# A diffusion step's head loop: the convolution's turned tiles in two PSUM banks instead of three, and pairs of w_ada moved to later places in the order

## Chip, cores and metric

One core of one Trainium2 chip runs the whole program. The metric is device microseconds of one execution, the median of three runs. An execution is also recorded by the hardware profiler; times "at 125.45" are microseconds from the start of the recorded span. Engines: PE (TensorE, matmuls and transposes), DVE (VectorE), ACT (ScalarE), POOL (GpSimd) and SP, which here only issues loads of weights.

## What is computed

One inference step of a two-layer diffusion trunk on 384 tokens (128 of context, 256 of a latent grid), width 1024, all in fp32. Cut to what matters:

```python
for l in range(DEPTH):                                   # 2 layers
    shift1, scale1, gate1, shift2, scale2, gate2 = split(silu(cond) @ w_ada[l] + b_ada[l])   # 6 x 1024, for c and c_ctx
    h = rms_norm(x) * (1 + scale1) + shift1
    q_lat, ckv, krope, conv_in, na_qkv = split(h @ w_in[l])
    o_mla = attention(8 heads of q_lat, ckv, krope)      # softmax
    o_conv = silu(layer_norm(depthwise_conv(glu(conv_in), width=31)))      # 256 channels
    o_na = neighbourhood_attention(4 heads of na_qkv)    # with a bias, softmax
    x = x + gate1 * (concat(o_mla, o_conv, o_na) @ w_out[l])
    h = rms_norm(x) * (1 + scale2) + shift2
    x = x + gate2 * grouped_moe(h)                       # 16 experts, two per token
```

## The kernel before, in words

**Order.** Every engine has its own program, written out by hand in the same order; semaphores join them. Nothing is scheduled at run time: an engine that waits holds back all that stands behind the wait in its program. Per layer the order is: norm, five stages of the input projection (`STAGES`, line 47), the first four heads turned (`turn_heads`, line 1019), then the **head loop** (PE: line 1194; ACT: 1751; DVE: 2361), then the output projection (`out_product`, 1234), the router and the experts.

**The head loop.** `GROUPS` (line 161) lists 12 heads: 8 of the latent attention, 4 of the neighbourhood one. The loop has 14 turns, i = 0 to 13. In turn i PE makes the scores of head i, turns the probabilities of head i-1 and multiplies the values of head i-2; DVE takes the maxima and normalises outputs; ACT does the exponentials and copies what PE turned. Some turns hold more: the second queries, keys and values (turn 0), further heads to be turned (3 and 7), the convolution's result turned (9, bank keys `cb`), its normalised rows turned back (11, keys `ln`), swish and first mixes (12).

**Pairs of w_ada.** The modulation's weights come in 24 pairs of 1 MB slots, 12 per layer. The first four pairs open the program. The other 20 (`LATER_PAIRS`, line 69; pairs 0 to 19 below) are fitted in between the first layer's work, since PE multiplies each with the two conditioning vectors and needs nothing else for it: `ADA_BEHIND` pairs behind each projection stage, `BEFORE_HEADS` ahead of the first heads, then one per turn (`pairs_after`, line 73; on PE `modulation`, line 1118, matmuls at line 1108). Before the change pairs 0 to 7 stand behind the stages, pair 8 before the heads, and pairs 9 to 19 in turns 0 to 10. Four pairs make a group in PSUM bank 7. When a group is full ACT copies it out (`evac_modulation`, line 1703, the copy at 1711); before or with the next pair PE turns it (`turn_group`, 1090, matmuls at 1096), and ACT copies the turned columns (1698). What is left at the end of the loop is closed by `close_modulation` (PE 1127, ACT 1691). Pairs 0 to 7 hold the rest of layer 0's modulation, 8 to 19 that of layer 1.

**The ring.** SP loads all weights in one fixed order (`ring_order`, line 124; issue at line 719) into six slots of SBUF: the load number q goes into the slot of load q-6 (before the experts) and waits until PE has used that up (`left`, line 642). The order in the ring is that in which PE uses the weights, so a pair that moves on PE moves in the ring. The four output weights OUT0 to OUT3 follow the last pair. Each is split into a high and a low part for PE: ACT's `out_high` (line 1653, cast at 1661) in the turns of `OUT_TURN` = (9, 10, 12, 12) (line 56), then DVE's `out_low` (2336, at 2339) from turn 11 on.

**PSUM banks.** `psum_plan` (line 207) lists all uses of a layer's first part in PE's order; they take the banks in rotation, seven in layer 0 (bank 7 belongs to the groups) and eight in layer 1 (line 304). PE writes a bank only when the use before it in that bank has been read (`once_free`). So a use that is dropped from the list moves every later one to another bank and behind another reader.

**The convolution.** DVE adds 31 taps (line 2278) into `conv_acc`, channels on partitions. In turn 9 PE turns it to tokens on partitions, three tiles of 128 tokens with 256 channels each, one bank per tile; DVE takes statistics (2403, 2405), POOL the root (762), and DVE normalises the three tiles from the same banks (`normalise_conv`, 2352, at 2357): in layer 0 at the end of turn 9, in layer 1 in turn 10 after the maxima.

Of the kernel before, what the change touches and what calls it, by code (L numbers as in the profile page):

```python
# [47 lines left out]
PAIRED = [js for js in STAGES if len(js) > 1]  # L48
PAIR_AT = [IN_AT[js[0]] for js in PAIRED]
PAIR_WIDTH = [sum(IN_WIDTH[j] for j in js) for js in PAIRED]  # L50
ADA_BEHIND = (2, 1, 2, 1, 2)
S_UP_AFTER = 3
OUT_SLOTS = D_MODEL // 256
OUT_PAIRS = OUT_SLOTS // 2
# [12 lines left out]

GROUP = 4
LATER_PAIRS = [(0, k) for k in range(4, PAIRS)] + [(n, k) for n in range(1, DEPTH) for k in range(PAIRS)]
AMONG_PROJ, BEFORE_HEADS = sum(ADA_BEHIND), 1  # L70


def pairs_after(n, what, i=0):
# [76 lines left out]
C_CTX, C_LAT = PAD, 2 * PAD + P  # L150
C_LEN = 3 * PAD + TOK
C_OUT = C_LEN - 2 * PAD

TAPS_BEFORE_LATENTS, TAPS_BEFORE_UP, TAPS_BEFORE_HEADS = 7, (18, 8), (21, 14)

# [51 lines left out]
def psum_plan(n):  # L207

    order = []
    open_group = []  # L210

    def pairs(which):

        for m, k in which:
            g, v = divmod(LATER_PAIRS.index((m, k)), GROUP)
            if v == 0:
                order.append(("group", g))
            order.extend([("turn", p) for p in open_group])
            open_group[:] = [g] if v == GROUP - 1 else []

    first_turns = [("n1", t, q) for t in range(2) for q in range(2)]
    if n == 0:

        for i, (m, k) in enumerate(FIRST_PAIRS):
            order += [("ada", m, k)]
            if i:
                order += [("mod", *FIRST_PAIRS[i - 1])]
            if i == len(FIRST_PAIRS) - 1:
                order += first_turns
        order += [("mod", *FIRST_PAIRS[-1])]  # L230
    else:
        order += first_turns
    for i, js in enumerate(STAGES):
        for t in range(TILES):
            order += [("proj", js[0], t)]
            if (i, t) == (0, 0):
                order += [("n1", 2, 0), ("n1", 2, 1)]
            if (i, t) == (2, 0):
                order += [("conv", 0), ("conv", 1)]
        pairs(pairs_after(n, "proj", i))  # L240
        if i == S_UP_AFTER:
            order += [("ql", 0), ("ql", 1), ("ckv",)]
            order += [("q", 0, t) for t in range(3)] + [("kv", 0, t) for t in range(4)]
    pairs(pairs_after(n, "heads"))
    order += heads_transposed(0)
    for i in range(len(GROUPS) + 2):
        if i < len(GROUPS):
            order += [("S", i, t) for t in range(3)]
        if i == 0:
            order += [("q", 1, t) for t in range(3)] + [("kv", 1, t) for t in range(4)]  # L250
        if 1 <= i <= len(GROUPS):
            order += [("PT", i - 1, 0), ("PT", i - 1, 1)]
        if i >= 2:
            order += [("O", i - 2)]
        if i == len(GROUPS):
            order += [("mix", t) for t in range(TILES)]
        if i == 3:
            order += heads_transposed(1) + [("rows",)]
        if i == 7:
            order += heads_transposed(2)  # L260
        if i == 9:
            order += [("cb", t) for t in range(3)]
        if i == 11:
            order += [("ln", 0), ("ln", 1)]
        pairs(pairs_after(n, "turn", i))
    order += [("turn", p) for p in open_group]
    order += [("out", 0, 0), ("mix", 3), ("mix", 4), ("out", 1, 0), ("shift",)]
    for t in range(1, TILES):
        for p in range(OUT_PAIRS):
            order += [("out", p, t)] + [(what, *k) for what, *k in AFTER_OUT[(t, p)] if what != "rest"]  # L270
    order += [("place",)]
    return order
# [93 lines left out]
def build(nc, wring, x_in, vec, rows, ckv_cache, kr_cache, nak_cache, nav_cache, cond, w_router,  # L366
          b_router, rope, shape_consts, na_bias, row_ids, no_token,
          y_prompt, y_sample, new_ckv, new_krope, new_nak, new_nav, h_rows, y_rows, tables, mod_dram):
    with ExitStack() as ctx:
# [253 lines left out]
        def bank_no(l, key):  # L623
            return USES[(l.n, *key)][0]
# [5 lines left out]
        def once_full(l, key):  # L630

            return bank_full[bank_no(l, key)], USES[(l.n, *key)][1] + 1

        def once_read(l, key):

            return bank_read[bank_no(l, key)], USES[(l.n, *key)][1] + 2
# [317 lines left out]
        def _(pe):  # L954

            def turn_around(l, key, parts, d=P):

                pe.wait_ge(*once_free(l, key))
                b = bank[bank_no(l, key)]
                for i, part in enumerate(parts):  # L960
                    mm = pe.transpose(b[0:d, i * P:(i + 1) * P], part, iden[:])  # L961
                mm.then_inc(bank_full[bank_no(l, key)], 1)
# [172 lines left out]
            for n in range(DEPTH):  # L1135
# [58 lines left out]
                for i in range(len(GROUPS) + 2):  # L1194
# [26 lines left out]
                    if i == 9:  # L1221

                        pe.wait_ge(sems["conv_done"], nth(l, "conv_done", 1))
                        for t in range(TILES):
                            at = 0 if t == 0 else C_LAT - PAD + (t - 1) * P
                            turn_around(l, ("cb", t), [conv_acc[:, c, at:at + P] for c in range(2)])
                    if i == 11:
                        pe.wait_ge(*once_read(l, ("cb", 2)))
                        for c in range(2):
                            turn_around(l, ("ln", c), [ln_tm[:, t, c * P:(c + 1) * P] for t in range(TILES)])  # L1230
                    modulation(l, pairs_after(n, "turn", i))
# [657 lines left out]
        def _(dve):  # L1889
# [337 lines left out]
            for n in range(DEPTH):  # L2227
# [114 lines left out]
                def mix_low(i):  # L2342
# [6 lines left out]
                        ins = dve.tensor_tensor(mixT_lo[1][:, i - 1, :], b[:, 0:TOK], mixT_hi[:, i + 3, :], ALU.subtract)  # L2349
                    ins.then_inc(bank_read[bank_no(l, ("mix", i))], 1)  # L2350

                def normalise_conv():
                    dve.wait_ge(sems["rstd_ready"], nth(l, "rstd_ready", RMS.index("conv") + 1))
                    for t in range(TILES):
                        dve.wait_ge(*once_full(l, ("cb", t)))
                        b = bank[bank_no(l, ("cb", t))]
                        dve.tensor_scalar(ln_tm[:, t, :], b[:, 0:CONV_CH], meanvar[:, t, 0:1], rstd[:, t:t + 1],
                                                ALU.subtract, ALU.mult) \
                                                    .then_inc(bank_read[bank_no(l, ("cb", t))], 1)

                for i in range(len(GROUPS) + 2):
                    if i < len(GROUPS):
# [35 lines left out]
                        out_low(3)  # L2398
                    if i == 9:
                        for t in range(TILES):  # L2400
                            dve.wait_ge(*once_full(l, ("cb", t)))
                            b = bank[bank_no(l, ("cb", t))]
                            dve.bn_stats(stats[:, t, :], b[:, 0:CONV_CH]).then_inc(sems["dve_step"], 1)
                            dve.wait_ge(sems["dve_step"], step(l))
                            dve.bn_aggr(meanvar[:, t, :], stats[:, t, :]).then_inc(sems["dve_step"], 1)
                            dve.wait_ge(sems["dve_step"], step(l))
                        dve.tensor_copy(ssum[:, 0:TILES], meanvar[:, :, 1]).then_inc(sems["dve_step"], 1)
                        dve.wait_ge(sems["dve_step"], step(l))
                        mean_squares(l, "conv", TILES, 1)
                        if n == 0:  # L2410
                            normalise_conv()
# [375 lines left out]
```

## Time and profile before

| what | value |
|---|---|
| median of 3 runs | 1071.9 us (1068.68 to 1073.7) |
| profiled execution, its own time | 1071.57 us |
| its span, first to last instruction | 1069.8 us |
| mean granted clock of TensorE | 0.97 |
| busy share of the span | PE 94%, DVE 39%, ACT 27%, POOL 13% |
| chain that ended last | PE 76%, DVE 9%, DMA 8%, ACT 3%, issue 2%, POOL 1% |
| HBM read | 307.08 MB |

How to read it: PE is busy nearly always, and most of the chain is its own work in the experts. The rest of the chain, DMA, DVE and ACT, lies in the two layers' first parts, some 0 to 294 us and 560 to 786 us. The granted clock is 1.00 for 2.4 GHz and 0.50 for 1.2 GHz; a value between is a stretch with both. In a timeline the durations of PE's matmuls overlap, so the queue's cost of a step is read from start to start.

### The profile page before, as it was taken

The numbers are of one execution on the slowest core, as the hardware profiler recorded it, in microseconds if no ns is written. First come the engines' busy times: TensorE is split into PE (matmuls) and PEld (weight loads), VectorE is DVE, ScalarE is ACT, GpSimd is POOL, SyncE is SP. The second block draws the span as 40 slices with busy tenths as digits, with TensorE's granted clock in tenths as the row PEclk, the third lists the DMA queues.
The fourth block names the chain that finished last, engine by engine and source line by source line (L and its number), as shares of the span: only waits on it lengthen the run. The fifth ranks groups of instructions, "written<-read, shape, count | busy, mean of one in ns | idle before, by whom it ended". The sixth has DMA issues, their size and how long they took to land.

```text
span 1069.8 us, 12824 instructions
## 1 busy us (share of the span) xinstructions
PE 1006.7 (94%) x4770; PEld 593.0 (55%) x4770; DVE 418.2 (39%) x861; ACT 290.9 (27%) x629; POOL 143.7 (13%) x192
## 2 busy tenths in 40 slices
PE   5899898999999999999979999889999999999975
PEld 1686556678854434444338976668874444343422
DVE  1348824586451010000136679767462100101014
ACT  2333265572111011010035337754210111101110
POOL 2200411201110000100101015201020110001000
PEclk9899989999899999999999999978999999999998
DMA  9778396864899999999981225104499999999971
GB/s 376 292 277 342 137 360 274 337 254 195 312 368 362 421 392 422 421 420 422 420 349 57 106 79 163 43 9 197 161 383 391 377 399 423 421 420 422 421 300 59
DMA packets 51376, 320.52 MB, mean 300 GB/s; under 512 B 8718, under 2 KB 8830, under 8 KB 16368
## 3 DMA queue, kind: packets, MB, share of 16 engines
q1 hardware_dynamic: 38448, 276.59, 63.9%
q0 software_dynamic: 12864, 43.08, 10.6%
q8 instruction: 40, 0.66, 0.2%
q14 instruction: 24, 0.20, 0.0%
HBM read 307.08 MB, written 21.25 MB: 307 GB/s over the span
## 4 chain that ended last, share of the span: by engine, by line
PE 76%; DVE 9%; DMA 8%; ACT 3%; issue 2%; POOL 1%; SPq 0%; DVEq 0%; POOLq 0%; ACTq 0%
PE bank L1372 26%; PE bank L1399 12%; PE bank L978 6%; PE bank L1249 5%; PE bank L996 4%; PE bank L961 3%; PE bank L1108 3%; DMA extra_ring<-wring_dram 3%; DMA y<-y_rows 2%; PE bank L1073 2%; PE bank L1039 2%; DMA ring<-wring_dram 2%; PE bank L968 2%; PE bank L1356 2%; PE bank L1285 1%
## 5 line engine op out<-in xcount | busy, mean ns | idle before, releaser
L1372 PE MATMUL bank<-ring,hgT 128*64 128x512 f32 (+1 forms) x512 | 156.4, 594 | 2.1 <-DMA ring<-wring_dram 1.6
L1372 PE MATMUL bank<-extra_ring,hgT 128*64 128x512 f32 (+1 forms) x512 | 155.9, 594 | 0.0
L1399 PE MATMUL bank<-extra_ring,hidT 128*64 128x512 f32 (+1 forms) x352 | 111.8, 624 | 9.7 <-DMA extra_ring<-wring_dram 9.7
L2533 DVE TENSOR_TENSOR sg<-bank,sg 128x512 f32<-128x512 f32 x22 | 15.2, 691 | 252.2 <-PE bank L1372 252.2
L1372 PEld LDWEIGHTS bank<-ring,hgT 128*64 128x64 f32 (+1 forms) x512 | 58.5, 157 | 87.5 <-issue 87.5
L1372 PEld LDWEIGHTS bank<-extra_ring,hgT 128*64 128x64 f32 (+1 forms) x512 | 58.3, 157 | 86.6 <-issue 86.5
L1399 PEld LDWEIGHTS bank<-extra_ring,hidT 128*64 128x64 f32 (+1 forms) x352 | 40.9, 163 | 71.4 <-issue 71.4
L2278 DVE SCALAR_TENSOR_TENSOR conv_acc<-conv_in,vecs,conv_acc 128x399 f32<-128x399 f32 x120 | 70.9, 632 | 2.1
L1108 PE MATMUL bank<-ring,cond_p 128*32 128x512 f32 x384 | 53.3, 675 | 17.0 <-DMA ring<-wring_dram 16.2
L978 PE MATMUL bank<-ring,hT 128*128 128x256 f32 x288 | 66.5, 392 | 2.6 <-DVE hT L1924 2.6
L889 POOL DMA_INDIRECT y_rows<-y,y_at x18 | 18.2, 1011 | 368.2 <-DVE y L2542 348.0
L762 POOL TENSOR_TENSOR rstd<-ms,half 128x28 f32<-128x28 f32 (+3 forms) x10 | 32.7, 3272 | 231.2 <-DVE ms L1900 231.2
L978 PEld LDWEIGHTS bank<-ring,hT 128*128 128x128 f32 x288 | 56.2, 197 | 11.6 <-DVE hT L1924 2.8
L1788 ACT COPY hgT<-bank 128x512 f32<-128x512 f32 x24 | 14.0, 585 | 167.3 <-PE bank L1356 140.4
L2542 DVE COPY y<-bank 128x512 f32<-128x512 f32 x18 | 12.4, 692 | 113.4 <-PE bank L1399 113.4
L1797 ACT ACTIVATE sg<-bank 128x512 f32<-128x512 f32 x22 | 13.1, 597 | 153.0 <-PE bank L1372 153.0
L1399 PE MATMUL bank<-ring,hidT 128*64 128x512 f32 (+1 forms) x160 | 49.6, 595 | 0.0
L1039 PE MATMUL bank<-kT,qT 96*128 96x128 f32 (+3 forms) x144 | 44.1, 441 | 0.2 <-ACT probsT L1648 0.2
L2018 DVE TENSOR_REDUCE rowmax<-bank 128x1 f32<-128x384 f32 (+1 forms) x56 | 24.8, 442 | 49.6 <-PE bank L1039 48.0
L1811 ACT COPY y<-bank 128x512 f32<-128x512 f32 x18 | 10.5, 585 | 107.6 <-PE bank L1399 107.6
L1249 PE MATMUL bank<-out_hi,mixT_hi 128*128 128x512 f32 x96 | 38.8, 404 | 1.1 <-DVE mixT_lo L2346 0.7
L1640 ACT ACTIVATE probs<-bank,negmax,qscale 128x384 f32<-128x384 f32 (+1 forms) x48 | 28.2, 594 | 34.9 <-DVE negmax L2021 34.8
(315 smaller groups left out, 1532.7 us busy)
## 6 DMA issues: line engine op xcount, KB each, us to landing
ring<-wring_dram SPq DMA_DIRECT2D x150, 1024.0 KB, 12.8
extra_ring<-wring_dram SPq DMA_DIRECT2D x108, 1024.0 KB, 17.8
y_rows<-hg POOLq DMA_DIRECT2D x6, 1024.0 KB, 6.2
kT<-mod_dram POOLq DMA_DIRECT2D x4, 1024.0 KB, 9.8
late<-y_rows POOLq DMA_DIRECT2D x4, 1024.0 KB, 15.5
ring<-wring_dram SPq DMA_DIRECT2D x4, 832.0 KB, 19.5
h_rows<-h_tok POOLq DMA_DIRECT2D x6, 512.0 KB, 6.2
ring<-wring_dram SPq DMA_DIRECT2D x4, 640.0 KB, 11.1
```

What stands on the lines that cost most here:

```text
L762: pool.tensor_tensor(rstd[:, 0:n], ms[:, 0:n], half[:].broadcast_to([P, n]), ALU.pow) \
L961: mm = pe.transpose(b[0:d, i * P:(i + 1) * P], part, iden[:])
L978: mm = pe.matmul(b[:, 0:n], hT[:, c, t * P:(t + 1) * P], w[:, c, :], start=(c == 0), stop=(c == KC - 1))
L996: mm = pe.matmul(b[:, 0:n], a, w, start=((c, k) == (0, 0)), stop=((c, k) == (KC - 1, 2)))
L1039: mm = pe.matmul(b[:, 0:hi - lo], qT[0:d, s, h, t * P:(t + 1) * P], kT[0:d, s, h, lo:hi], start=True, stop=True)
L1108: mm = pe.matmul(bank[b][32 * i:32 * (i + 1), :], cond_p[:, s % 2 * 4 + i, at:at + 32], w[:, i, :], start=first, stop=last)
L1249: mm = pe.matmul(b[:, :], a, w, start=((c, k) == (0, 0)), stop=((c, k) == (KC - 1, 2)))
L1372: mm = pe.matmul(b[lo:hi, :], hgT[:, 4 * i + c, lo:hi], in_ring(l, expert_slot(place, s + i))[:, c * 512:(c + 1) * 512], start=((i, c) == ...
L1399: mm = pe.matmul(b[m][lo:hi, :], hidT[:, u % 2, 2 * i + c, lo:hi], in_ring(l, expert_slot(place, 4 + i))[:, at:at + 512], start=((i, c) == ...
L1640: act.activation(out, b[:, 0:hi - lo], ACT.Exp, bias=negmax[:, g, t:t + 1], scale=qscale[:, p, 4 * t + h:4 * t + h + 1] if p < 2 else 1.0, ...
L2018: dve.tensor_reduce(rowmax[:, t:t + 1], b[:, 0:n], AX, ALU.max).then_inc(sems["dve_step"], 1)
L2278: ins = dve.scalar_tensor_tensor(conv_acc[:, c, :], conv_in[:, c, k:k + C_OUT], tap, conv_acc[:, c, :], ALU.mult, ALU.add)
```

## The change

In layer 0 the pairs are placed otherwise. One pair instead of two stands behind the fifth stage (pair 6), none before the heads, and pairs 7 to 19 stand in turns 0 to 12. So pair 7 goes from the fifth stage to turn 0, pair 8 from before the heads to turn 1, and each of pairs 9 to 19 two turns later than before. Groups close and are turned later with them: group 1 (pairs 4 to 7) is turned in turn 1 instead of before the heads, group 2 in turn 5 instead of 3, group 3 in turn 9 instead of 7, group 4 after the loop as before, but it is full only in turn 12 instead of 10. In the ring the loads move alike. `OUT_TURN` stays.

In both layers the convolution's three turned tiles take two banks: tiles 0 and 1 share `cb 0`, tile 2 has `cb 1`. PE's six transposes and DVE's work are the same; DVE waits for the bank of the tile, and frees the first bank after tile 1, the second after tile 2.

```diff
-ADA_BEHIND = (2, 1, 2, 1, 2)
+ADA_BEHIND = (2, 1, 2, 1, 1)
...
-AMONG_PROJ, BEFORE_HEADS = sum(ADA_BEHIND), 1
+AMONG_PROJ, BEFORE_HEADS = sum(ADA_BEHIND), 0
...
+CONV_ROWS = (0, C_LAT - PAD, C_LAT - PAD + P)
...
         if i == 9:
-            order += [("cb", t) for t in range(3)]
+            order += [("cb", 0), ("cb", 1)]
...
                         pe.wait_ge(sems["conv_done"], nth(l, "conv_done", 1))
-                        for t in range(TILES):
-                            at = 0 if t == 0 else C_LAT - PAD + (t - 1) * P
-                            turn_around(l, ("cb", t), [conv_acc[:, c, at:at + P] for c in range(2)])
+                        for k, ts in enumerate(((0, 1), (2,))):
+                            turn_around(l, ("cb", k), [conv_acc[:, c, CONV_ROWS[t]:CONV_ROWS[t] + P] for t in ts for c in range(2)])
                     if i == 11:
-                        pe.wait_ge(*once_read(l, ("cb", 2)))
+                        pe.wait_ge(*once_read(l, ("cb", 1)))
...
+                def turned_conv(t):
+                    dve.wait_ge(*once_full(l, ("cb", t // 2)))
+                    return bank[bank_no(l, ("cb", t // 2))][:, t % 2 * CONV_CH:(t % 2 + 1) * CONV_CH]
+
                 def normalise_conv():
                     dve.wait_ge(sems["rstd_ready"], nth(l, "rstd_ready", RMS.index("conv") + 1))
                     for t in range(TILES):
-                        dve.wait_ge(*once_full(l, ("cb", t)))
-                        b = bank[bank_no(l, ("cb", t))]
-                        dve.tensor_scalar(ln_tm[:, t, :], b[:, 0:CONV_CH], meanvar[:, t, 0:1], rstd[:, t:t + 1],
-                                                ALU.subtract, ALU.mult) \
-                                                    .then_inc(bank_read[bank_no(l, ("cb", t))], 1)
+                        ins = dve.tensor_scalar(ln_tm[:, t, :], turned_conv(t), meanvar[:, t, 0:1], rstd[:, t:t + 1],
+                                                ALU.subtract, ALU.mult)
+                        if t:
+                            ins.then_inc(bank_read[bank_no(l, ("cb", t - 1))], 1)
...
                         for t in range(TILES):
-                            dve.wait_ge(*once_full(l, ("cb", t)))
-                            b = bank[bank_no(l, ("cb", t))]
-                            dve.bn_stats(stats[:, t, :], b[:, 0:CONV_CH]).then_inc(sems["dve_step"], 1)
+                            dve.bn_stats(stats[:, t, :], turned_conv(t)).then_inc(sems["dve_step"], 1)
```

## Rows read from the trace of the kernel before

**Rows 1.** Chain that ended last, in order of time, layer 0: start us, us, what.
```profile
125.45 0.33 SPq L719
...
125.83 8.69 DMA ring<-wring_dram
...
134.56 1.93 PE bank L1108 x8
...
138.30 4.48 PE bank L961 x28
...
155.60 0.33 PE bank L961 x3
```
**Rows 2.** Stretches: us, busy PE, PEld, DVE, ACT, POOL, PEclk, DMA share, GB/s.
```profile
130.00:134.50 4.50, 1.06 (x8) 0.16 (x8) 2.75 (x5) 0.00 (x0) 4.50 (x10) 0.97 1.03 360
136.00:142.00 6.00, 6.00 (x35) 5.45 (x32) 0.00 (x0) 2.69 (x7) 0.00 (x0) 0.58 1.00 318
694.00:696.00 2.00, 2.00 (x10) 1.44 (x11) 0.36 (x1) 2.00 (x6) 0.00 (x0) 0.50 0.94 383
714.00:726.00 12.00, 12.00 (x48) 10.19 (x48) 5.71 (x12) 4.87 (x12) 0.00 (x0) 0.50 0.00 0
```
**Rows 3.** Timeline, layer 1: start us, us, engine, line, operation [idle before, its releaser].
```profile
693.32 4.07 PE L961 MATMUL bank<-shapes,qk 128*64 128x128 f32 x18 [1.44 <-ACT probs L1640]
...
711.96 1.45 DVE L2357 TENSOR_SCALAR squares<-bank,meanvar,rstd 128x256 f32<-128x256 f32 x3
...
712.64 1.51 PE L1073 MATMUL bank<-proj,probsT 128*128 128x64 f32 x6 [2.93 <-DVE squares L2357]
...
715.79 3.35 PE L1039 MATMUL bank<-kT,qT 64*128 64x128 f32 x6
...
727.02 1.28 ACT L1770 ACT_TABLE_LOAD   x1
```
**Rows 4.** Timeline, layer 0, around the first heads and turns.
```profile
120.70 12.12 DVE L2278 SCALAR_TENSOR_TENSOR conv_acc<-conv_in,vecs,conv_acc 128x399 f32<-128x399 f32 x20
...
125.35 3.64 PE L1108 MATMUL bank<-ring,cond_p 128*32 128x512 f32 x32
...
153.38 1.78 PE L1039 MATMUL bank<-kT,qT 96*128 96x128 f32 x6
...
177.67 1.06 PE L1096 MATMUL bank<-four,xn 128*128 128x8 f32 x8
```
**Rows 5.** Line 719, the six ring loads issued from 125 to 130 us: issue to landing.
```profile
DMA to landing us min/median/max: 4.7/13.4/20.0
```
**Rows 6.** Line 719, the two ring loads issued from 210 to 215 us (OUT0, OUT1).
```profile
DMA to landing us min/median/max: 4.8/5.6/6.4
```
**Rows 7.** Timeline, layer 0, turns 8 to 13 and the start of the output projection.
```profile
211.28 1.92 PE L1108 MATMUL bank<-ring,cond_p 128*32 128x512 f32 x16
...
219.70 1.91 ACT L1661 CAST out_hi<-ring 128x2048 fp32r<-128x2048 f32 x1
...
224.40 1.93 PE L1108 MATMUL bank<-ring,cond_p 128*32 128x512 f32 x16
...
225.88 0.37 ACT L1640 ACTIVATE probs<-bank,negmax 128x128 f32<-128x128 f32 x1 [4.27 <-DVE negmax L2023]
226.25 1.78 PE L1039 MATMUL bank<-kT,qT 64*128 64x128 f32 x6
...
230.55 0.39 ACT L1640 ACTIVATE probs<-bank,negmax 128x128 f32<-128x128 f32 x1
...
233.95 1.28 ACT L1770 ACT_TABLE_LOAD   x1
...
238.45 0.48 PE L1249 MATMUL bank<-out_hi,mixT_hi 128*128 128x512 f32 x1
...
241.76 0.26 ACT L1698 COPY modT<-bank 128x16 f32<-128x16 f32 x2
...
244.16 0.47 PE L1249 MATMUL bank<-out_hi,mixT_hi 128*128 128x512 f32 x1 [0.67 <-DVE mixT_lo L2346]
```

## The prediction

> **What bounds the kernel now.** I read the chain of waits in order of time first, then the granted clock by stretches, then the timelines of the stretches that the change touches. The first layer has one long hole. PE ends the last projection at 125.4 us; SP issues the next ring loads at 125.45, because their slots held that projection's weights; and PE is on the chain again only at 134.56, with the second half of pair 8 [rows 1]. The reader should see two prices there: 8.69 us of waiting for a load, and behind it 28 transposes that take 4.48 us, where three take 0.33 elsewhere [rows 1]. The clock says why: through the hole PE is busy 1.06 of 4.5 us, and from 136 to 142 it is granted 0.58, most of it the lower level (1.2 GHz) [rows 2]. The second layer has a smaller hole: PE waits 2.93 us in turn 10 for the convolution's normalised tile on DVE [rows 3], and runs at 0.50 from 714 to 726 [rows 2].
>
> **Part 1: the early wait goes.** Today pairs 6 and 7 take 3.64 us from 125.35, so a pair costs 1.85 of PE's queue (its 1.92 in a timeline overlaps its neighbours) [rows 4]. Afterwards only pair 6 stands before the first heads, and its load is already there: PE is free at 127.2. The 28 transposes no longer follow a hole, so I price them at the full clock, 28 x 0.11 = 3.1 us (bounds 3.1 and today's 4.48 [rows 1]): 130.3. The scores of turn 0, queries and keys keep today's 8.9 us (they start 0.2 before the heads' modelled end, 138.30 + 4.48, and end where pair 9 starts, 153.38 - 1.85 [rows 1, 4]): 139.2. Pair 7 now stands there, so turn 1's scores start at 141.05 against 153.38, a lead of **12.3 us**. Group 1's turn (8 matmuls, 1.06 [rows 4], some 1.0 of PE's queue) moves from before the heads into turn 1: lead 11.3. Groups 2 and 3 are turned two turns later as well, so the lead swings between 11.3 and 12.3, which changes no sum; ACT's copy of each group moves with it, into its idle time. The cover: DVE ends its taps at 132.8 [rows 4], 1.9 us after the first scores would be ready; queries and keys (7.3 us) hide that. Without them 1.9 would be lost.
> Four ring loads leave at 125.45 to 127.5 instead of six. Six needed 4.7 to 20.0 us to land [rows 5]; pair 8's second half is wanted 18 us after its issue, pair 9's later. Lower bound: the slowest, 2 us lost; I take none, since two of the six are gone. SP's order is otherwise the same, and nothing on POOL's queue moves.
>
> **Part 2: the output weights come late.** This is the added wait. OUT0 is loaded into the slot of pair 17's first half. Today that is turn 8: the pair starts at 211.28 [rows 7], the load leaves 1.1 us later and lands in 4.8 us, OUT1 behind it in 6.4 [rows 6], and ACT's split of OUT0 in turn 9 starts at 219.70 without a wait [rows 7]. The split stays in turn 9, but pair 17 goes to turn 10. Then:
> - ACT reaches the split at 219.70 - 12.3 = 207.4.
> - Pair 17 starts where pair 19 does today, 224.40 - 11.3 = 213.1 [rows 7]; issue 214.2; landed 219.0. ACT stands **11.6 us** (13.2 by the slower landing; I take the faster, as OUT0 is again the first of its two).
> - Queued behind it on ACT: the copy of group 3's turn (0.25), the exponentials of turn 10, OUT1's split. The split and the copy end at 221.1; those exponentials start at 225.88 today [rows 7]. The lead left is 4.8.
> - Who waits: PE. Turn 11's first scores get the bank of group 3's turn, which ACT reads only then. PE idles from 214.9 to 221.1, 6.2 us.
>
> **Part 3: what moved to turns 11 and 12.** At the full clock: turn 11's scores start at 221.1, their exponentials 4.3 us later as today (226.25 to 230.55 [rows 7]): 225.4, lead 5.1. The probabilities are there at 226.95; pair 18 now lies ahead of their transposes and ends at 226.2 + 1.85 = 228.05 instead, so the lead is 4.2. OUT2 and OUT3, issued behind pair 18 at 227.3 and 228.3, land at 232.1 and 234.7, just in time for ACT. Pair 19 hides in turn 12 behind ACT. But group 4's copy now stands behind all of ACT's splits and copies, which end at 241.76 today [rows 7]: 237.5, and a copy of 512 columns (a quarter of a split's 1.91), 238.0. PE must turn the group (1.0) before the output projection, which so starts at 239.1 against 238.45; its second block starts at 244.2 against 244.16 [rows 7]. **At the full clock the whole lead is spent: 0.**
> The clock is the unknown. A 6.2 us hole is longer than the one behind which the rows show 0.58. If turn 11 runs at the lower level for as long as that stretch (some 7 us), pair 18 starts 2.6 us later (scores 1.65, transposes 0.85, values 1.0, less 0.9 of waits that were there), and the second block at 246.9: +2.7. If the fall lasts until pair 18 is done (rest of the values and transposes, the pair's 1.85 twice): +6.0. PE's 2.9 us wait for group 4 (its values end at 235.2) can start another fall under the output projection: half of 7 us, 0 to +3.4. So the first layer gives 0 to +9.4; I take **+4**, nearest to the 136 to 142 row: 2.7, and 1.3 for the second fall.
> The first two loads of expert weights leave after pair 19, so two turns later; they are wanted only after the router, a whole output projection on: 0.
>
> **Part 4: two banks.** The six transposes, the statistics and the normalising stay; only bank and release change. In the first layer that is nothing (0.1 us: the first statistics wait for four transposes instead of two). In the second, where no pairs are, the rotation of eight is one step shorter: the values in turn 10 get the bank of turn 9's values, long read, instead of the convolution's first tile. They start 2.93 us earlier, at 709.7 [rows 3]. But the next scores now take the convolution's banks, the first free after the second normalised tile, 711.96 + two thirds of 1.45 = 712.9 [rows 3]. The wait moves and shrinks from 2.93 to 1.8; the scores start at 713.0 against 715.79 [rows 3], 2.8 sooner. If the clock still falls, the rest keeps its pace: 2.2 to 2.8 gained. If it stays full, layer 0's own distance from these scores to the table load of the swish holds, 226.25 to 233.95 = 7.7 us [rows 7]: 720.7 against 727.02 [rows 3], 6.3 gained. A wait of 1.44 us was already followed by 0.50 in this layer [rows 2, 3], so I take **-2.5**.
> The Trainium skill (TensorE: Matmul & The Clock Gate, HAM oscillation) has the clock fall after gaps that are long enough, and so it would rather keep it in the second layer: that result is the 6.3 just worked out. The trace's 1.44 us case speaks against it.
>
> **Sum.** The profiled execution took 1071.57 us, its span 1069.8 and 1.8 around it; it lies 0.3 below the median of 1071.9. 1071.57 + 4 - 2.5 + 0.3 = 1073.4; I say **1073**.
>
> **Rivals.**
> - *Slower.* ACT's wait for OUT0 drags a long low clock with it; this decides from the point where the fall outlasts pair 18. +9.4 - 2.2 = +7: 1079. For it: in the second layer the low clock held for 12 us of the same small matmuls (0.50 from 714 to 726 [rows 2]). Against: pairs 18 and 19 are long dense matmuls that layer 1 doesn't have. 0.25.
> - *Faster.* The clock holds in the second layer and recovers at once in the first: 0 - 6.3, 1065.5. For it: the remaining wait is 1.8 instead of 2.93. Against: the 1.44 us case. 0.13. The Trainium skill's rule (same page and section) would make this the outcome for the second layer, though not for the first.
> - *It doesn't do what it says.* The early wait returns in turn 1, because pair 8's second half lands after 20 us or more [rows 5]: 2 to 3 us of the lead lost, 1076. For it: the small bias loads share the engines then. Against: two megabytes less in front. 0.07.
>
> **How the numbers follow.** About 0.5% (5.4 us) is what a measurement of this kernel can tell from no change. My forecast (0.55) and the third rival (0.07) lie within it: 0.62 the same, 0.13 faster, 0.25 slower. The range leaves out part of each outer rival, under a fifth in all: 1066 to 1080.
>
> **What would show it.** Right: no PE wait after the last projection in layer 0, turn 1's scores near 141; ACT idle over 10 us before OUT0's split, released by the ring's load; PE idle some 6 us before turn 11's scores and a low clock behind; in layer 1 the wait in turn 10 gone from the values and standing before turn 11's scores. Wrong: ACT not waiting for OUT0 at all (then over 7 us faster); pairs 7 to 9 waiting for their loads; the output projection of layer 0 starting before 235 or after 249.

## The result, and the profile after

The change made the kernel **slower**: 1079.26 us, median of 8 runs, against 1072.7 us for the kernel before, run beside it; ratio 1.0069, 95% interval 1.0036 to 1.0102. The time lies in the forecast's range (1066 to 1080), but the forecast was 1073, within what a measurement can tell from no change. What came is the rival called *Slower*, which gave 1079.

| | before | after |
|---|---|---|
| profiled execution, its own time | 1071.57 us | 1079.59 us |
| its span | 1069.8 us | 1077.7 us |
| mean granted clock | 0.97 | 0.964 |
| end of the last projection (start of pair 6) to the first expert matmul of layer 0 | 173.94 us | 182.97 us |
| that expert matmul to layer 1's first projection | 270.79 us | 271.56 us |
| from there to the first expert matmul of layer 1 | 221.02 us | 220.03 us |

The program before pair 6 is the same in both, and yet pair 6 starts at 125.35 in one profile and at 124.57 in the other. So layer 0 is measured from pair 6 on: it lost 9.03 us. Layer 1 won 0.99; the stretch between lost 0.77; what stands ahead of pair 6 and behind layer 1's first expert gave back 0.78 and some 0.1. The sum is 7.9, the difference of the spans. **The loss lies in layer 0, and 7.9 of it in the head loop**, before the output projection starts (113.10 us from pair 6 before, 120.99 after).

The chain of the changed kernel, turns 10 to 12 of layer 0 (start us, us, what), shows it:

```profile
212.49 1.04 PE bank L1109 x8
213.53 0.02 issue
213.54 4.85 DMA ring<-wring_dram
...
218.41 0.03 ACT out_hi L1661
...
220.22 0.25 ACT modT L1698 x2
220.47 0.14 issue
220.60 3.32 PE bank L1040 x6
...
229.77 3.06 PE bank L1109 x16
232.84 0.02 issue
232.85 7.54 DMA ring<-wring_dram
240.39 0.02 issue
240.41 1.90 ACT out_hi L1661
242.31 0.97 ACT mixT_hi L1667 x2
243.28 0.50 ACT xn L1711
243.78 0.04 issue
243.82 1.88 PE bank L1097 x8
245.70 5.91 PE bank L1249 x18
```

Read it downwards. Pair 17's first half ends at 213.53; only then does OUT0 leave; ACT splits it at 218.41, copies group 3's turn, and PE starts turn 11's scores at 220.60. PE's work behind that takes longer (3.32 us instead of 1.78 for the six score matmuls, 3.06 instead of 1.93 for a pair [rows 7]). The last output weight leaves at 232.85, behind that slow pair, and takes 7.54 us. ACT splits it, copies the mixes, copies group 4 at 243.28, and only then can PE turn group 4 and begin the output projection. The waits at these places and the one in layer 1, from the timeline of the same kernel (start us, us, engine, line, operation, idle before and its releaser):

```profile
218.41 1.90 ACT L1661 CAST out_hi<-ring 128x2048 fp32r<-128x2048 f32 x1 [11.35 <-DMA ring<-wring_dram]
...
220.60 3.32 PE L1040 MATMUL bank<-kT,qT 64*128 64x128 f32 x6 [6.26 <-ACT modT L1698]
...
243.82 1.88 PE L1097 MATMUL bank<-four,xn 128*128 128x8 f32 x8 [3.74 <-ACT xn L1711]
...
245.56 0.77 PE L1249 MATMUL bank<-out_hi,mixT_hi 128*128 128x512 f32 x1
...
252.02 0.47 PE L1249 MATMUL bank<-out_hi,mixT_hi 128*128 128x512 f32 x1
...
722.30 2.39 PE L1040 MATMUL bank<-kT,qT 64*128 64x128 f32 x6 [2.55 <-DVE squares L2359]
```

The output projection of layer 0 starts at 245.56 against 238.45 [rows 7], its second block at 252.02 against 244.16. And the clock, by stretches (us, busy PE, PEld, DVE, ACT, POOL, granted clock, DMA share, GB/s):

```profile
125.00:130.00 5.00, 5.00 (x47) 3.78 (x40) 4.86 (x9) 3.27 (x8) 4.44 (x9) 1.00 0.87 308
214.50:220.50 6.00, 0.00 (x0) 0.00 (x0) 0.00 (x0) 2.09 (x4) 0.00 (x0) 0.83 0.96 350
221.00:232.00 11.00, 11.00 (x45) 7.27 (x48) 6.54 (x13) 6.16 (x15) 0.00 (x0) 0.50 0.00 0
243.00:249.00 6.00, 5.18 (x16) 4.50 (x17) 4.29 (x4) 1.02 (x4) 0.00 (x0) 0.50 1.02 430
724.00:736.00 12.00, 12.00 (x57) 11.39 (x56) 6.94 (x13) 7.35 (x14) 0.00 (x0) 0.50 0.00 0
```

The early hole of 125 to 134 us [rows 1, 2] is gone: PE is busy 5.00 of 5 us at the full clock. In its place stand a hole of 6 us at 214.5, eleven busy microseconds at 1.2 GHz behind it, and a second stretch at 1.2 GHz under the output projection. In layer 1 the wait has moved from the values to the scores, and the low clock behind it is there as before.

### The profile page after: what moved, and what is told of

Read it like the earlier page. It is cut to its first block, busy times and chain, and to the rows that moved or that the text cites. A ratio compares the mean times of both kernels' runs of the same rounds, so it can differ in the third digit from the quotient of the medians.

```text
span 1077.7 us, 12824 instructions
## 1 busy us (share of the span) xinstructions
PE 1010.4 (94%) x4770; PEld 598.8 (56%) x4770; DVE 418.0 (39%) x861; ACT 291.0 (27%) x629; POOL 143.7 (13%) x192
## 4 chain that ended last, share of the span: by engine, by line
PE 78%; DMA 9%; DVE 7%; ACT 3%; issue 2%; POOL 1%; SPq 0%; DVEq 0%; POOLq 0%; ACTq 0%
PE bank L1372 26%; PE bank L1399 12%; PE bank L1249 6%; PE bank L979 6%; PE bank L997 4%; PE bank L1109 4%; PE bank L962 4%; DMA extra_ring<-wring_dram 3%; PE bank L1040 3%; PE bank L1074 3%; DMA y<-y_rows 2%; DMA ring<-wring_dram 2%; PE bank L969 2%; PE bank L1356 2%; PE bank L1285 1%
## 5 line engine op out<-in xcount | busy, mean ns | idle before, releaser
L1249 PE MATMUL bank<-ring_lo,mixT_hi 128*128 128x512 f32 x96 | 38.3, 399 | 0.0
## 6 DMA issues: line engine op xcount, KB each, us to landing
kT<-mod_dram POOLq DMA_DIRECT2D x4, 1024.0 KB, 10.8
```

Of the source, the lines that this page charges most:

```text
L1249: mm = pe.matmul(b[:, :], a, w, start=((c, k) == (0, 0)), stop=((c, k) == (KC - 1, 2)))
```

## The experiments

The theory: ACT's wait for OUT0 makes PE's hole, the hole brings a low clock that lasts through pair 18, and the copy of group 4, last in ACT's queue, turns that delay into a second hole. The rivals: the late places of pairs 18 and 19 cost it whatever ACT waits for; the hole's own microseconds are lost, not the clock's; the shared PSUM bank costs it. Dummy matmuls are matmuls whose result nobody reads, into a free bank. The table is read from each kernel's profile: from pair 6's start to the first matmul of the output projection and to the first expert matmul (layer 0), and from layer 1's first projection to its output projection. The last two columns are timed runs against the kernel before, run beside each of them; the profiles are one of each kernel.

| kernel | pair 6 to output projection | to first expert | layer 1 | ratio | 95% interval |
|---|---|---|---|---|---|
| before | 113.10 | 173.94 | 161.38 | | |
| after | 120.99 | 182.97 | 159.64 | 1.0069 | 1.0036 to 1.0102 |
| two banks alone | 113.23 | 174.09 | 158.21 | 1.0012 | 0.9972 to 1.0053 |
| moved pairs alone | 121.29 | 183.26 | 167.32 | 1.0048 | 1.0020 to 1.0076 |
| split one turn later | 110.94 | 172.83 | 156.65 | 0.9958 | 0.9917 to 0.9999 |
| 44 dummy matmuls | 118.19 | 179.96 | 159.19 | 1.0028 | 0.9985 to 1.0071 |
| 26 dummy matmuls | 114.26 | 176.15 | 166.76 | 1.0023 | 0.9988 to 1.0058 |
| group 4 copied early | 116.91 | 176.93 | 158.89 | 0.9991 | 0.9956 to 1.0026 |
| 26 dummies and early copy | 111.44 | 172.93 | 158.31 | 0.9941 | 0.9908 to 0.9973 |
| pairs one place later | 104.47 | 164.23 | 168.53 | 0.9910 | 0.9876 to 0.9944 |
| pairs doubled in turns 3, 5 | 102.31 | 163.15 | 158.82 | 0.9872 | 0.9812 to 0.9932 |
| doubled, layer 1 filled | 102.28 | 163.13 | 154.08 | 0.9804 | 0.9762 to 0.9847 |
| the same again | 102.25 | 163.12 | 155.20 | 0.9795 | 0.9763 to 0.9826 |
| the same, three banks | 102.25 | 163.18 | 154.36 | 0.9810 | 0.9780 to 0.9841 |

Layer 0 repeats to 0.3 us between kernels with the same order of pairs and splits (before and two banks alone; after and moved pairs alone; the last four rows). Layer 1 does not: with one and the same code its column runs from 156.65 us (split one turn later) to 168.53 us (pairs one place later). So an edit of layer 0 is read from the first two columns, and a single span says little.

### One part of the change at a time

```diff
-ADA_BEHIND = (2, 1, 2, 1, 1)
+ADA_BEHIND = (2, 1, 2, 1, 2)
...
-AMONG_PROJ, BEFORE_HEADS = sum(ADA_BEHIND), 0
+AMONG_PROJ, BEFORE_HEADS = sum(ADA_BEHIND), 1
```

*Two banks alone* is the changed kernel with these lines back; *moved pairs alone* is the kernel before with the two changed lines and its three banks.

> The two-bank convolution alone, pairs of w_ada where they were before. Theory (all of the loss comes from the moved pairs in layer 0): layer 0 as before (output projection near 238.5 us), in layer 1 the scores of turn 11 wait 2 to 2.6 us in place of the values of turn 10 and the output projection starts 1.5 to 2.5 us sooner; in all 1 to 2.5 us faster than before, ratio 0.998. Rival (the shared bank costs time): 2 us or more slower than before, ratio 1.002 or more.

> The moved pairs alone, three banks for the convolution. Theory: layer 0 as in the changed kernel (ACT stands over 10 us before OUT0's split, PE idle 6 us before turn 11's scores, output projection near 245.5 us, second block near 252), layer 1 as before; 8 to 10 us slower than before, ratio 1.008. Rival (the convolution's banks cost it): within 2 us of before, ratio 1.000 to 1.002.

Layer 0 came as the theory said: 0.15 us from before with the banks alone, 9.3 us lost with the pairs alone. Layer 1's output projection came 3.2 us sooner with the banks alone (158.21 against 161.38), which is well within what that layer varies by with one code. In time the two banks alone can't be told from no change (1.0012, where a gain of 0.2% was expected). The interval leaves room for the rival's 1.002, but the trace shows no stage that the shared bank made longer. The pairs alone cost 0.48% on that chip, less than the 0.8% expected. Their layer 1, expected "as before", took 167.32 us; the section on the hardware comes back to that.

### The root: ACT's wait for OUT0

```diff
+OUT_TURN_FIRST = (10, 11, 12, 12)
...
-                        if OUT_TURN[j] == i:
+                        if (OUT_TURN if n else OUT_TURN_FIRST)[j] == i:
```

> The changed kernel, in layer 0 the split of OUT0 one turn later (turns 10, 11, 12, 12). Theory (ACT's wait for OUT0 in turn 9 is the root): ACT waits at most 3 us for OUT0, PE has no hole before turn 11's scores and keeps the full clock there, pair 18 starts near 221 us, not 229.7; group 4's copy, still behind all splits, ends near 235 and the output projection starts at 236 to 237; 9 us faster than the changed kernel, 2 to 4 us faster than before, ratio 0.997. Rival (the late places of pairs 18 and 19 cost it, whatever ACT waits for): output projection still at 244 or later, ratio 1.005 or more.

Half a miss. From its timeline (ACT's split, then PE):

```profile
221.52 1.90 ACT L1662 CAST out_hi<-ring 128x2048 fp32r<-128x2048 f32 x1 [2.68 <-DMA ring<-wring_dram]
...
223.83 0.55 PE L963 MATMUL bank<-shapes,squares 128*128 128x128 f32 x3 [1.85 <-ACT probs L1641]
224.31 2.91 PE L1110 MATMUL bank<-ring,cond_p 128*32 128x512 f32 x16
...
237.77 1.06 PE L1098 MATMUL bank<-four,xn 128*128 128x8 f32 x8 [2.60 <-ACT xn L1712]
```

ACT waits 2.68 us instead of 11.35 and the 6 us hole is gone, as expected; but the split now holds up turn 11's exponentials, PE waits 1.85 us for them, and pair 18 runs at the low clock again (2.91). Measured from pair 6 the output projection is 10 us sooner than in the changed kernel, so the late places of the pairs don't make the loss whatever ACT waits for, and that rival (1.005 or more) fell. They do eat most of the lead: with the pairs one turn earlier than here (*one place later* than before, below) the output projection comes another 6.5 us sooner.

### The hole or the clock

```diff
+                    if n == 0 and i == 11:
+                        keep_busy(l, ("S", 11, 2), 26)
                     if i < len(GROUPS):
                         scores(l, i)
```

The first of these two kernels has 44 in place of 26.

> The changed kernel with 44 dummy matmuls of 128 columns ahead of turn 11's scores in layer 0 (some 5.2 us at the full clock, in a bank that is free), so that PE works through the hole while ACT still waits for OUT0. Theory (the hole costs by the low clock behind it): turn 11 and pair 18 at 1.00, pair 18 done near 228 instead of 232.8, the fourth output weight landed by 235.5, output projection near 239 to 240, second block near 245; 6 us faster than the changed kernel, within 2 us of before, ratio 0.999. Rival (the hole's own 6.2 us are lost whatever the clock): output projection at 244 or later, time as the changed kernel, ratio 1.006.

> The changed kernel with 26 dummy matmuls ahead of turn 11's scores in layer 0. One cost 0.229 us with 44 of them, so these end near 220, when the scores can start; with 44 they ended 3.5 us too late. Theory (the low clock behind the hole is what the sum had too small): turn 11 at 1.00 from 220, pair 18 near 225.5 to 227.3, the fourth output weight landed by 234, output projection near 238.5, second block near 244.5, so layer 0 as before within 1 us and 7 us faster than the changed kernel. Rival (something else in turns 11 and 12 holds PE up): pair 18 at full clock, but output projection still at 241 or later.

With 44 the dummies took 10.09 us (213.68 to 223.70), not 5.2: one takes 0.23 us and stands as two matmuls in the trace, and I had their price wrong by a factor of two. PE came 4 us too late to its own work, since ACT had read group 3's turn by 219.82. One of the 12 runs of this kernel took 4249 us; it is not in the ratio, and why it did is not known. With 26, by the timeline of PE:

```profile
214.73 6.07 PE L969 MATMUL bank<-shapes 128*128 128x128 f32 x52
221.02 1.82 PE L1040 MATMUL bank<-kT,qT 64*128 64x128 f32 x6 [0.22 <-ACT modT L1700]
...
226.24 1.92 PE L1109 MATMUL bank<-ring,cond_p 128*32 128x512 f32 x16
...
238.23 1.06 PE L1097 MATMUL bank<-four,xn 128*128 128x8 f32 x8 [2.76 <-ACT xn L1713]
239.14 0.48 PE L1251 MATMUL bank<-out_hi,mixT_hi 128*128 128x512 f32 x1
```

and by stretches:

```profile
214.50:220.50 6.00, 6.00 (x55) 5.78 (x52) 0.00 (x0) 1.67 (x1) 0.00 (x0) 1.00 0.88 343
221.00:232.00 11.00, 10.81 (x86) 8.00 (x90) 7.54 (x15) 9.76 (x22) 0.00 (x0) 1.00 0.32 117
239.00:243.00 4.00, 4.00 (x13) 3.19 (x13) 3.68 (x4) 0.25 (x2) 0.00 (x0) 0.57 1.00 424
```

The hole is as long as in the changed kernel (turn 11's scores start 96.1 us behind pair 6 in this one, 96.0 in that one), PE only works through it, and the 11 us behind it are granted 1.00 instead of 0.50. The output projection starts at 239.14, 6.7 us sooner from pair 6 than in the changed kernel. ACT's wait for OUT0 is still there and still eats the lead that the early wait had left; **of the 7.9 us that the change lost beyond that lead up to the output projection, the low clock behind the hole was 6.7.** That rival (the hole's own microseconds) fell. The timed ratio (1.0023) is 0.5% better than the change's, though the intervals overlap.

### The copy that stands last

```diff
                             out_high(l, j)
+                            if (i, j) == (len(GROUPS), 2):
+                                evac_modulation(l, pairs_after(n, "turn", i))
...
-                    evac_modulation(l, pairs_after(n, "turn", i))
+                    if i != len(GROUPS):
+                        evac_modulation(l, pairs_after(n, "turn", i))
```

> The changed kernel, ACT's copy of group 4 between the splits of OUT2 and OUT3 instead of behind all copies of turn 12. Theory (of the 7.9 us, a good half lies in PE's 3.7 us wait for that copy and in the low clock behind it): the copy ends near 240.2 instead of 243.8, the output projection starts near 241 to 241.5 instead of 245.6, second block at 246 to 247 instead of 252; 5 us faster than the changed kernel. Rival (ACT's last mixes end at the same time and hold the second block): output projection sooner, second block still at 250 or later.

> The changed kernel with both repairs, 26 dummy matmuls ahead of turn 11's scores and group 4's copy between the splits of OUT2 and OUT3 (layer 0). Theory (two causes that add up: the low clock behind the hole, 6.5 us, and the copy that stands behind all of turn 12 on ACT): no low clock from 205 to 260, output projection near 236.5, second block near 242, 10 us sooner than the changed kernel and 2 us sooner than before. Rival (the early copy only shifts the wait to ACT's mixes once the clock is full): second block at 244 or later, as with the filler alone.

Both as the theory said. With the copy alone (ACT at 240.71, split of the last weight at 242.09) the output projection starts 4.1 us sooner from pair 6 and the first expert 6.0, with the same low clock of turn 11 ahead of it. With both repairs there is no low clock between 164 and 260 us, the second block starts at 239.93, and layer 0 is 1.0 us shorter than before, ratio 0.9941. The rival (ACT's mixes hold the second block) fell.

### Where the pairs go

*One place later* puts pair 7 back behind the fifth stage (`ADA_BEHIND` ends in 2, `BEFORE_HEADS` stays 0). *Doubled* keeps the change, but gives turns 3 and 5 two pairs each, in turn 3 the first ahead of its heads, so that pairs 17 to 19 are in turns 8 to 10 again:

```diff
+DOUBLED = (3, 5)
...
-    count = ADA_BEHIND[i] if what == "proj" else BEFORE_HEADS if what == "heads" else 1
+    count = ADA_BEHIND[i] if what == "proj" else BEFORE_HEADS if what == "heads" else 1 + (i in DOUBLED)
+    if what == "turn":
+        first += sum(d < i for d in DOUBLED)
...
                     if i == 3:
...
+                        modulation(l, pairs_after(n, "turn", i)[:1])
                         turn_heads(l, 1)
...
-                    modulation(l, pairs_after(n, "turn", i))
+                    modulation(l, pairs_after(n, "turn", i)[i == 3:])
```

> The changed kernel with pair 7 behind the fifth stage again, so that each of pairs 8 to 19 is one place, not two, later than before (turns 0 to 11). Theory: the early wait is gone all the same (lead 9.5 us); ACT waits some 4.6 us for OUT0, but group 3's turn is then read in turn 8, ahead of the split, so PE has no hole before turn 11's scores and keeps the full clock; group 4's copy stands in turn 11, ahead of the last splits; output projection near 231, 6 to 8 us faster than before, ratio 0.993. Rival (any pair past turn 10 costs the lead): output projection at 238 or later, ratio 1.000 or more.

> The changed kernel, but two pairs in turn 3 (the first ahead of its heads, where PE waits 2.3 us for ACT) and two in turn 5, so that pairs 17, 18 and 19 stand in turns 8, 9 and 10 again as before. Theory (the early wait removed is worth its 12 us, and only the two places at the end gave it back): ACT does not wait for OUT0, turn 11 at the full clock, output projection of layer 0 near 227 to 229, 10 us faster than before, 17 us faster than the changed kernel, ratio to before 0.990. Rival (the ring can't bring the pairs any faster, the early wait only made up for it): PE waits for loads of pairs between turns 3 and 8, and the output projection starts at 234 or later.

Both as expected, and both beat the kernel before. One place later, ACT waits for OUT0 all the same, but PE does not, and group 4's copy, now in turn 11, waits only 0.47 us for pair 19. Timeline of ACT:

```profile
212.90 1.90 ACT L1661 CAST out_hi<-ring 128x2048 fp32r<-128x2048 f32 x1 [4.37 <-DMA ring<-wring_dram]
...
222.15 0.59 ACT L1711 COPY xn<-bank 128x512 f32<-128x512 f32 x1 [0.47 <-PE bank L1109]
```

The scores of turn 11 follow pair 18 at 214.75 without a wait, since group 3's turn was read a turn earlier. With doubled pairs ACT splits OUT0 at 207.43 with no wait, and the whole loop runs at 2.4 GHz, as the row of this one stretch shows (columns as above):

```profile
120.00:230.00 110.00, 106.87 (x740) 69.40 (x739) 68.47 (x149) 66.87 (x163) 22.86 (x27) 1.00 0.87 330
```

The lead is kept to the end: the output projection starts 10.8 us sooner from pair 6 than before. Not all of that is the early wait's. In turn 3 PE now waits 0.96 us for ACT instead of 2.35, and the 25 transposes behind that wait take 3.57 us instead of 4.90; turn 3 was not doubled without turn 5, so the shares are not known. The ring brings thirteen pairs in eleven turns at a DMA share of 0.87; PE waits for none of them.

### Layer 1 at the full clock

```diff
+                    if n and i == 11:
+                        keep_busy(l, ("PT", 10, 0), 11)
...
                     if i == 7:
+                        if n:
+                            keep_busy(l, ("qT", 2, 0), 8)
                         turn_heads(l, 2)
```

> The kernel with two pairs in turns 3 and 5, and in layer 1 dummy matmuls where PE waits: 8 ahead of the heads of turn 7 (before its 1.44 us wait for ACT) and 11 ahead of turn 11's scores (before the 2.55 us wait for the convolution's banks). Theory (in layer 1 too the waits cost by the low clock behind them, which differs from run to run): the clock stays at 1.00 through turns 7 to 12, the scores of turn 11 still start when the normalised tile is out, and the output projection of layer 1 starts 151 to 153 us after the layer's first projection, against 157.0 with the same pairs and 159.6 in the changed kernel; 4 to 6 us faster than the kernel with doubled pairs, ratio to before 0.982. Rival (the waits themselves are the cost): 157 us again or more, ratio 0.987.

> The kernel with doubled pairs and dummy matmuls in layer 1, but with three banks for the convolution; the 11 dummy matmuls stand ahead of the values of turn 10, where PE waits with three banks. Theory (the two banks are worth 2.5 us in layer 1 once the clock does not hide it): layer 1's output projection starts 155 to 156 us after the layer's first projection, against 152.7 with two banks; 2 to 3 us slower than the same kernel with two banks. Rival (the wait only moves, nothing is won): 153 us and the same time within 1 us.

> The kernel with doubled pairs, two banks and dummy matmuls in layer 1 once more, to stand beside the one with three banks on the same chip. Theory: as its first run, 152 to 153 us from layer 1's first projection to its output projection, ratio to before 0.980 to 0.983, and 2 to 3 us faster than three banks. Rival: as three banks within 1 us.

With PE kept at work through the two waits the clock stays at 1.00 from 681 to 715 us in all three. From turn 8's scores to the output projection layer 1 now takes 27.2 us with two banks, in both runs. The same pairs without dummies take 30.7:

```profile
685.96 1.77 PE L1044 MATMUL bank<-kT,qT 64*128 64x128 f32 x6
...
716.65 0.48 PE L1254 MATMUL bank<-out_hi,mixT_hi 128*128 128x512 f32 x1
```

From the first projection on it is 154.08 and 155.20 us against 158.82, 4.7 and 3.6 less. That is not the 151 to 153 expected; the 157.0 of that expectation had left out the first 1.8 us of the projection. The runs stand closer together too: 1051.5 to 1057.49 us, against 1052.9 to 1069.26. The two banks are worth less than I expected. Scores of turns 8 and 11, two banks (the second run):

```profile
685.47 1.77 PE L1044 MATMUL bank<-kT,qT 64*128 64x128 f32 x6
...
701.34 1.92 PE L1044 MATMUL bank<-kT,qT 64*128 64x128 f32 x6
...
712.64 0.47 PE L1258 MATMUL bank<-out_hi,mixT_hi 128*128 128x512 f32 x1
```

and three banks:

```profile
685.79 1.77 PE L1043 MATMUL bank<-kT,qT 64*128 64x128 f32 x6
...
702.77 1.78 PE L1043 MATMUL bank<-kT,qT 64*128 64x128 f32 x6
...
713.94 0.47 PE L1258 MATMUL bank<-out_hi,mixT_hi 128*128 128x512 f32 x1
```

From turn 8's scores to the output projection it is 27.17 us with two banks and 28.15 with three: 1.0 us, not 2 to 3. From the first projection on nothing of it is left: three banks (154.36) lie between the two runs with two. The clock ahead of turn 8 differs between these profiles (from 655 to 665 us 1.00 with three banks, 0.91 and 0.86 with two). The medians stand 2.1 us apart (1052.85 and 1054.95), with intervals that overlap. So the theory was too large, and the rival ("the same") misses the 1.0 us behind turn 8, which rests on one profile with three banks.

## Why the prediction was wrong, by its own steps

**Part 1 held.** PE does not wait behind the last projection; heads' transposes 3.19 us (3.1 said), turn 1's scores at 140.29, 15.72 us behind pair 6 (15.70 said). No pair waits for its load, so the third rival fell.

**Part 2 held.** ACT stands 11.35 us before OUT0's split (11.6), PE idles 6.26 us (6.2), turn 11's scores start at 220.60 (221.1), turn 10's exponentials at 220.35 against 225.88 [rows 7]: counted from pair 6 a lead of 4.75 (4.8). The added wait was found, with its size and with all that queues behind it.

**Part 3 at the full clock held.** The sum had the output projection at 239.1; the kernel with 26 dummy matmuls, which is the change without the low clock behind the hole, starts it at 239.14 (113.75 said and 114.26 measured from pair 6). The whole lead is spent, and 1.2 us more (0.65 said).

**The step that failed is the term for the low clock in Part 3.** I took +2.7 because the stretch of 136 to 142 us [rows 2] lasted some 7 us. This one lasted twice that: 0.83 already in the idle stretch, 0.50 through 221 to 232, until pair 18 was nearly over. The bound I had worked out for just that, +6.0, is what happened; measured against the kernel with the dummies it is 6.7. The second fall was sized rightly: I took 1.3 for it, and with the dummies, where only this fall is left, the second block stands 6.4 us behind the first (239.14 to 245.52) where the sum at the full clock had 5.1. With 6.7 in place of 2.7 the first layer's term is 8.0; the second block came 7.9 us later than before, 8.6 counted from pair 6. My argument against a long fall, that pairs 18 and 19 are long dense matmuls, did not hold: pair 18 itself ran at the low clock nearly to its end (0.50 up to 232, the pair from 229.77 to 232.83), and OUT3's load left only when it was done (232.85, landed 7.5 us later where I had 6.4).

**Part 4: the mechanism held, the size did not.** The wait went from the values to the scores (2.55 us, 1.8 said). Turn 8's scores and the output projection before, then turn 8's scores after:

```profile
697.32 1.80 PE L1039 MATMUL bank<-kT,qT 64*128 64x128 f32 x6
...
731.46 0.47 PE L1249 MATMUL bank<-out_hi,mixT_hi 128*128 128x512 f32 x1
```

```profile
706.36 1.85 PE L1040 MATMUL bank<-kT,qT 64*128 64x128 f32 x6
```

Turn 11's scores start 15.94 us after turn 8's (722.30) instead of 18.47 (715.79 [rows 3]), 2.5 sooner (2.8 said). The clock fell all the same, as I assumed. Of the gain 1.7 us is left at the output projection and 1.0 at the first expert, against 2.5; these are single profiles of a layer that varies by more. Part of that 2.5 was clock as well: where the clock held, turn 11's scores come 15.87 us after turn 8's with two banks and 16.98 with three, 1.1 apart. The 6.3 us of the rival *Faster* was nearly all clock: from turn 8's scores to the output projection the kernel before took 34.14 us (697.32 to 731.46), three banks at the full clock take 28.15, 6.0 less without any edit of the banks, and two banks take off the last 1.0. The 7.7 us from turn 11's scores to the table load that I carried over from layer 0 came out exactly where the clock held (701.34 to 709.04).

**The weighing.** 8.0 - 1.0 is the rival *Slower* (+9.4 - 2.2) almost to the microsecond, and its deciding point was named: a fall that outlasts pair 18. It had 0.25 against 0.55. That its sum fits so well is partly luck: both of its terms were too large (9.4 for 8.0, 2.2 for 1.0), and the clock was back just before pair 18 ended. What should have tipped it stood in the rows: of the two stretches at 0.50 that I read, the 12 us of rows 2 ran over the same scores, transposes and values as turn 11; the 7 us had the heads' transposes in it.

The Trainium skill (TensorE: Matmul & The Clock Gate, HAM oscillation) has the clock fall behind PE's long gaps. For the 6.26 us gap the trace agrees (0.50 behind it). That rule does not tell of the shorter ones here: the clock fell to 0.50 behind 2.55 us in layer 1, and behind 1.85 us in the kernel with the later split.

## What to carry to other kernels

A load that takes over a slot is late by as much as the slot's last reader was moved: before a step is put off, look up which load stands behind it in the ring and who waits for that in order. A hole of PE is priced by the low clock behind it, and its length is taken from a stretch with the same steps, not from some other fall: the falls here lasted from 3 to 37 us. A few dummy matmuls in the hole tell in one run how much of the loss was clock. Here the early wait could be removed at a gain by moving the work to other turns, one of which (turn 3) has a wait of PE anyway, with the last pairs left where they were. And where single profiles of one stage differ by 12 us, an edit is read from the nearest common step.

## What the runs showed of the hardware

The same wait before the same transposes is followed by very different clocks. In turn 7 of layer 1 PE waits 1.44 us for ACT before 18 transposes, in every kernel without dummies there. These are the transposes with two banks alone, from the timeline:

```profile
695.11 3.01 PE L962 MATMUL bank<-shapes,qk 128*64 128x128 f32 x18 [1.44 <-ACT probs L1640]
```

and the 18 us from there on by the clock:

```profile
695.00:713.00 18.00, 15.98 (x105) 11.91 (x105) 13.51 (x41) 12.22 (x33) 1.97 (x3) 1.00 0.21 66
```

The same transposes with the moved pairs alone, whose layer 1 is that of the kernel before:

```profile
701.16 3.91 PE L961 MATMUL bank<-shapes,qk 128*64 128x128 f32 x18 [1.44 <-ACT probs L1640]
```

and the 37 us behind them:

```profile
703.00:740.00 37.00, 36.22 (x130) 27.89 (x131) 18.32 (x52) 16.82 (x43) 0.87 (x1) 0.50 0.02 8
```

Full clock in one, 37 us at 1.2 GHz in the other, and some 3 us in the kernel before, whose layer 1 has the same code as the second (4.07 for the 18 transposes [rows 3], 0.50 from 694 to 696 [rows 2]). Such falls go with the 12 us by which layer 1 differs between profiles of one code: the slowest (pairs one place later) is granted 0.50 to 0.59 in each 10 us from 685 to 725, the fastest (split one turn later) 0.66 to 1.00. They also go with most of the 20 us by which 35 runs of the kernel before differ in one session (1066.69 to 1086.68). The timed runs have no trace, but each has its mean granted clock, 0.973 in the fastest and 0.948 in the slowest, and time and clock go together over the 35 (correlation -0.92). In which stage the clock fell in them isn't shown. The Trainium skill (TensorE: Matmul & The Clock Gate, What's actually happening) says that how many matmuls run cold at a kernel's start varies from run to run of one kernel; these rows show a like spread in mid-kernel.

PE's arrival at pair 6 differed as well, from 122.46 to 127.74 us, with the same program up to there. Why isn't settled by these runs.
